# The rwkv scan's masked blocks: five VectorE operations per chunk and direction in place of one on GpSimd

## What is computed

```python
def rwkv7_scan(r, w, k, v, a, b):
    def step(state, xs):
        r_t, w_t, k_t, v_t, a_t, b_t = xs
        sa = jnp.einsum('bhvk,bhk->bhv', state, a_t)
        state = state * w_t[:, :, None, :] + sa[..., None] * b_t[:, :, None, :] + v_t[..., None] * k_t[:, :, None, :]
        return state, jnp.einsum('bhvk,bhk->bhv', state, r_t)
    _, y = lax.scan(step, jnp.zeros((bsz, heads, hd, hd), jnp.float32), xs)
```

## Time and profile before

| | us |
|---|---|
| median of three executions | 7314.83 |
| lowest, highest | 7311.81, 7324.32 |
| the profiled execution's own time | 7314.5 |
| its span in the trace | 7313.0 |
| the scan's part of that span | about 1303 to 1850 |

### The profile page before, as it was taken

The page is one execution under the profiler, slowest core; times in us unless marked ns, Lnnn a source line. Parts: engine busy times, 40 slices in busy tenths (PEclk is TensorE's granted clock), DMA queues, the critical chain, the costliest instruction groups (busy, mean ns, idle before and its releaser), DMA issues. The chain is left out here.

```text
span 7313.0 us, 91107 instructions
## 1 busy us (share of the span) xinstructions
PE 5559.0 (76%) x35960; PEld 4054.5 (55%) x35960; DVE 3337.4 (46%) x4351; ACT 1158.3 (16%) x1848; POOL 522.1 (7%) x320
## 2 busy tenths in 40 slices
PE   6878871789266886688788679958459777779988
PEld 4668870689144774333334458732435445658876
DVE  8436658434545655644344442234244445532233
ACT  2102223122202001300000210011013223211100
POOL 0000002212000000222121000002000000000000
PEclk8989985899688987599899889976557669989999
DMA  1221113330221442330422022224210111322233
GB/s 67 84 84 32 34 50 151 119 96 10 108 95 49 173 149 83 134 123 26 156 80 99 30 85 95 94 86 118 81 37 5 22 31 32 111 100 74 69 121 121
DMA packets 269336, 605.70 MB, mean 83 GB/s; under 512 B 33548, under 2 KB 132747, under 8 KB 268092
## 3 DMA queue, kind: packets, MB, share of 16 engines
q1 hardware_dynamic: 195416, 415.86, 17.3%
q10 hardware_dynamic: 57696, 128.47, 4.6%
q0 software_dynamic: 15968, 57.78, 2.2%
HBM read 409.84 MB, written 192.19 MB: 82 GB/s over the span
## 5 line engine op out<-in xcount | busy, mean ns | idle before, releaser
L385 PE MATMUL gu_ps<-kept_h_hi,gu_w_hi 128*128 128x512 f32 x704 | 275.2, 391 | 39.7 <-DVE gu_w_lo L118 39.7
L2050 PE MATMUL lc_ps<-lc_tabi,lc_z 128*128 128x512 f32 x512 | 229.5, 611 | 69.3 <-issue 69.3
L385 PE MATMUL gu_ps<-kept_h_lo,gu_w_hi 128*128 128x512 f32 x704 | 274.9, 390 | 0.0
L385 PE MATMUL gu_ps<-kept_h_hi,gu_w_lo 128*128 128x512 f32 x704 | 274.8, 390 | 0.0
L385 PE MATMUL win_ps<-kept_hn_hi,win_w_hi 128*128 128x512 f32 x576 | 224.9, 391 | 39.7 <-DVE win_w_lo L118 39.7
L385 PE MATMUL win_ps<-kept_hn_lo,win_w_hi 128*128 128x512 f32 x576 | 224.7, 390 | 0.0
L385 PE MATMUL win_ps<-kept_hn_hi,win_w_lo 128*128 128x512 f32 x576 | 224.6, 390 | 0.0
L2036 PE MATMUL lc_ps<-lc_v,lc_tab 128*128 128x512 f32 x512 | 222.3, 592 | 0.0
L2050 PEld LDWEIGHTS lc_ps<-lc_tabi,lc_z 128*128 128x128 f32 x512 | 100.4, 197 | 198.4 <-issue 198.2
L385 PE MATMUL wo_ps<-wo_x_hi,wo_w_hi 128*128 128x512 f32 x384 | 154.4, 402 | 60.7 <-DVE wo_x_lo L118 59.9
L420 DVE COPY win_o<-win_ps 128x1024 f32<-128x1024 f32 x36 | 44.1, 1225 | 285.6 <-PE win_ps L385 285.6
(11 more groups left out here) (631 smaller groups left out, 13627.8 us busy)
## 6 DMA issues: line engine op xcount, KB each, us to landing
rk_in<-s_decayed SPq DMA_DIRECT2D x8, 3072.0 KB, 15.9
oproj_mod_w<-in_ada_w POOLq DMA_DIRECT2D x12, 2048.0 KB, 9.3
gu_w<-in_w_gu SPq DMA_DIRECT2D x44, 512.0 KB, 3.5
win_w<-in_w_in SPq DMA_DIRECT2D x36, 512.0 KB, 3.5
s_z<-win_o ACTq DMA_DIRECT2D x36, 512.0 KB, 2.6
s_decayed<-rkp_ring SPq DMA_DIRECT2D x32, 512.0 KB, 2.7
dn_kv<-s_qkv SPq DMA_DIRECT2D x16, 768.0 KB, 6.1
wo_w<-in_w_out SPq DMA_DIRECT2D x24, 512.0 KB, 4.5
```

The source lines that it names most:

```text
L385: mm = pe.matmul(ps[:, u, h, :], a, b, start=(k == 0 and n == 0), stop=(k == kt - 1 and n == len(pairs) - 1))
L2050: mm = pe.matmul(ps[:, 0, 2 * (ct % 2) + e, :], z[:, kind, ft, ct * P:(ct + 1) * P], tabi[:, kind, ft, :], start=(n == 0), stop=(n == 7))
```

## The change

GpSimd's list for this stage is removed. VectorE makes each of the blocks 1 to 5 with an operation of its own, one level ahead of its use: both level 1 blocks stand behind the two `sd` operations and ahead of the level loop, and inside the loop the block of level l + 1 stands ahead of the sums of level l of the same direction. The semaphore `off_rest` now counts five per chunk, and TensorE's `level_y` waits for the count of its own level.

```diff
-            @block.gpsimd
-            def _(pool):
-                pool.wait_ge(const_in, 64)
-                for i in range(RCH):
-                    for d in range(2):
-                        pool.wait_ge(per[d]["aa_ready"], i + 1)
-                        pool.wait_ge(per[d]["y_done"], i * LV)
-                        pool.tensor_tensor(off[d][:, 1:, :, :],
-                                           turns[d][i % 2]["aa"][:, first, :].unsqueeze(1).to_broadcast([P, LV - 1, RPAIRS, RH]),
-                                           masks[:, d, 1:, :].unsqueeze(2).to_broadcast([P, LV - 1, RPAIRS, RH]),
-                                           ALU.mult).then_inc(per[d]["off_rest"], 1)
-
@@ tensor: level_y
-                        pe.wait_ge(s["off_rest"], i + 1)
+                        pe.wait_ge(s["off_rest"], i * (LV - 1) + l)
@@ vector: ahead of the masked aa
-                            dve.wait_ge(s["off_rest"], i - 1 if i else 0)
+                            if i >= 2:
+                                dve.wait_ge(s["off_rest"], (i - 1) * (LV - 1))
@@ vector: behind sd
+                    def later_off(d, l):
+                        s = per[d]
+                        dve.wait_ge(s["aa_ready"], i + 1)
+                        if i:
+                            dve.wait_ge(s["y_done"], (i - 1) * LV + l + 1)
+                        dve.tensor_tensor(off[d][:, l, :, :], turns[d][i % 2]["aa"][:, first, :], pairs(masks[:, d, l, :]),
+                                          ALU.mult).then_inc(s["off_rest"], 1)
+
+                    for d in range(2):
+                        if inner:
+                            later_off(d, 1)
                     for l in range(1, LV):
                         for d in range(2):
                             s, b, t = per[d], bufs[d], turns[d][i % 2]
                             A, Y, DD, G = banks[d]
                             if inner:
+                                if l + 1 < LV:
+                                    later_off(d, l + 1)
                                 dve.wait_ge(s["z_done"], i * (LV - 1) + l)
                                 dve.wait_ge(s["x_ready"], i * XN + 2 * l)
```

## The result

| | before | changed |
|---|---|---|
| median, 22 executions each | 7316.55 us | 7324.52 us |
| lowest, highest | 7303.27, 7327.52 | 7316.61, 7337.22 |
| profiled execution's span | 7313.0 | 7331.3 |
| scan: first memset to last state sum, in those profiles | 545.4 | 555.8 |

The ratio is 1.0014, with a 95% interval of 1.0007 to 1.0020: 0.14% slower, some 10 us (5 to 15). 7335 us, +20.2 us, was forecast. The two profiled spans differ by 18 us, but only 10.4 us of that lie in the scan; the rest is in stages that the change does not touch, and single executions of either kernel spread over more than 20 us.

A forecast was written before the change was run, and what follows sets the result against it. TensorE's list was taken to bound the scan. 16.4 us of stalls at level 1 plus 3.8 us within the loop made 20.2 us on 7314.5 us, 7334.7, predicted as 7335 us; range 7326 to 7348.

The forecast's parts named there:

- What bounds the stage: Scan, 1338 to 1850 us: TensorE's list sets the pace, busy 476.87 of 512 us; GpSimd is off the path.
- Removed: nothing: 32 GpSimd operations of 3110 ns mean disappear; nothing waited for them, so worth nothing, the shorter VectorE operations included.
- the rival that built on it, at 7300 us: Front of each chunk: VectorE operations freed from GpSimd's hold-up bring TensorE's y(0) forward, 15 us at most; chance 0.04.
- The stall at level 1: Head of the level loop: TensorE's y(0) waits 1.20 us for the new block in 14 chunks, 0.7 us in chunk 0.
- The blocks in the loop: Levels 2 to 4: direction 1's block delays its `x` by 0.08 us, 3.8 us over 16 chunks; level 1 nothing.
- dense VectorE: New blocks on VectorE start a whole duration, 0.42 us, apart instead of 0.33 us; +29, 7344 us; chance 0.16.
- the upper sum: Total with 0.42 us start spacing on VectorE: y(0) stalls 1.29 us, `x` is delayed 0.24 us; 29.3 us.
- a granted clock below 1.00 in the stage: Sign in the changed kernel's profile: TensorE's granted clock under 1.00 in the scan would make the prediction wrong.
- I find no slack in which the 1.20 us could go: Level 1: everything queued behind y(0) on TensorE shifts with it, so each of 14 chunks pays 1.20 us in full.
- only chunk 9 gives 1.1 us back: Chunk 9's issue gap of 1.14 us just behind level 1 absorbs stall: 17.5 us less 1.1 gives 16.4 us.
- chunk 0's 0.7: Chunk 0, without `sd` and `read_state`: z of level 1 starts at 1340.49 in place of 1339.83, costing 0.7 us.
- Absorbed: TensorE's issue gaps shrink after it has stood still, so part of the stalls comes back; +7, 7322 us; chance 0.13.

The follow-up runs named there:

- lock_kept: Changed kernel with GpSimd still doing its old operation, into a spare tile nobody reads; ratio to the kernel before 1.0028 (1.0016-1.0040).
- loop_only: Changed kernel with GpSimd making the level 1 block alone, VectorE levels 2 to 5 inside the loop; ratio to the kernel before 0.9999 (0.9990-1.0008).
- in_gaps2: Changed kernel with all blocks still on VectorE, moved to places where it waits anyway; ratios to the kernel before 1.0003 and, timed again, 0.9991.
- longer_stall: Changed kernel with four more VectorE operations, into a spare tile, ahead of the level 1 blocks in each turn; ratio to the kernel before 1.0059 (1.0042-1.0076).

## Why the prediction was right in its parts, and where it was off

**What bounds the stage** held: TensorE's list does, and GpSimd was off the path.

**Removed: nothing** held. The level 0 block got 0.30 us shorter on the mean, and lock_kept shows that this is worth nothing on the path. The rule on the shared port from the Trainium skill (SBUF — State Buffer, section Who interferes with whom) describes a real hold-up, and its removal gained no time: the rival that built on it, at 7300 us, is refuted.

**The stall at level 1** was sized at 1.20 us and is 1.11 us. That it falls on every chunk but chunk 5 held: 15 waits for the new block, the one of chunk 0 among them.

**The blocks in the loop** were sized at 0.08 us, three to a chunk; they are 0.07, shown alone by loop_only. VectorE's start spacing stayed at 0.33 us with two semaphore waits in front of each block, so dense VectorE, 7344 us, is refuted. With it falls the upper sum, 29.3 us, which I had set beside what the Trainium skill says in VectorE: DVE Perf Modes, section on the TRN2 errata.

**The clock.** I had named a granted clock below 1.00 in the stage as a sign against the prediction. From 1338 to 1850 us it is 0.99 in the changed kernel's profile. It fell to 0.50 twice there (near 1497 and 1630 us), both times beside an issue gap of 2.7 or 2.8 us in a turn with an input load. The kernel before has such a fall too, once in its first profile (1625 us) and four times in its second, so it does not come from the change.

**The step that failed** is "I find no slack in which the 1.20 us could go", with its consequence that only chunk 9 gives 1.1 us back. For the part from the first `sd` on, the forecast's terms are 20.2 less chunk 0's 0.7 and 0.24, some 19.3 us. Measured, as the mean of two profiles on either side, are 491.4 - 478.3 = 13.1 us (10.7 to 15.5, as the kernel before scatters). By turns: the ten without loads cost 10.0 us where the forecast has 10 x 1.44 = 14.4; the four load turns 2.0 us where it has 3 x 1.20 + 4 x 0.24 - 1.1 = 3.5 (chunk 5 without a stall); the last 1.1 in place of 1.4. Of the 4.4 us missing in the ten, 0.9 is the size of the terms (1.35 in place of 1.44), and 3.5 us are small issue gaps that the stall took in, 0.35 us a turn. The second number leans on the two profiles of the kernel before; beside in_gaps2, whose even turn is the same 30.40 us and whose excess is 0.24 and 0.27 us, it would be 0.2 us a turn. Chunk 0 seems to have given its stall back too: the time from the stage's start to the first `sd` is 64.4 and 64.7 us in the changed kernel beside 64.7 and 66.0.

I had this mechanism as the rival *Absorbed*, and weighed against it that most chunks show no issue gap over 0.7 us. That was the wrong test. Gaps of 0.2 us and less do not show as idle time of TensorE, since a product's record is 0.22 us long, while the products start some 0.035 us apart: the product at 1422.65 starts 0.22 us behind the one before it, and its idle time is given as 0.01 us. The right reading was in the trace: of the ten turns without loads in the kernel before, eight are longer than 30.5 us, up to 31.88 us, although every turn has the same work. The 132.5 us that I gave for the issue gaps were no measure either: 19.7 us of them are waits of the products. So the direction, the places and the price of each part were right, and the total was too high by what the gaps take in. The truth lies between the forecast and this rival: some 10 us (5 to 15) in place of 20. The median, 7324.5 us, is 1.5 us under the low end of the range, 7326 us, which the interval of the ratio straddles; the range reached so far down only because it was drawn toward this rival. That the change makes the kernel slower is clear of the scatter. But I gave 0.80 to slower by more than 0.2%, and 0.14% is on the other side of that line, where I had put 0.17.

## What to carry to other kernels

A stall on the bounding engine costs less than its length where that engine's list also has irregular issue gaps, so look at how even its turns are before counting a stall once per turn: here the first 0.4 us or so of stall in each turn was free (the excess was 0.24 to 0.52 us in the four profiles with a turn of 30.40 us), and the rest cost its full length, and 1.55 us more where the clock fell. Moving an operation to a half-idle engine is a matter of its place in that engine's list: the same 160 operations cost some 13 us of stage where TensorE waits for them or for the sums behind them, and nothing that these runs can tell in the waits that VectorE had already. And where executions scatter by 20 us, compare the stage by its shortest turn, which came out the same to 0.01 us in each repetition, after a look at whether it is also the usual one.

## What the runs showed of the hardware

- Beside 11 of 15 waits of 2.6 us and more (longer_stall) TensorE's granted clock fell to 0.50, beside the other 4 it stayed at 1.00, and it stayed there after waits of 0.92 us (changed kernel, chunk 8). A fall cost 1.55 us, nearly as much as the longer wait itself (35.01 in place of 33.46 us).
- TensorE's instructions came in packets of 16 KB, one for each 127 products with their weight loads, 4.05 to 4.2 us apart and 6.5 to 7.7 us while the input loads ran. Where the products caught up with them, TensorE stood still until 1.2 to 1.6 us behind a packet's end (kernel before, both profiles).
- A VectorE operation with two SBUF inputs (the level 0 block) took 0.42 us alone and up to 1.14 us while GpSimd read SBUF; this returned when GpSimd's operation was put back, even with nobody reading its result.
- VectorE started independent 128x256 operations 0.33 us apart, though each took 0.42 us, also with two fulfilled semaphore waits between them. Where each waited for the one before (longer_stall), four took 1.80 us.
